# Output tiles between the block products of four feed-forward blocks, in six short stretches

## The reference

```python
def swiglu(x, w_in, w_out):          # x 512x1024, w_in 1024x5632, w_out 2816x1024
    gate, up = jnp.split(x @ w_in, 2, axis=-1)
    return (jax.nn.silu(gate) * up) @ w_out
x = x + 0.5 * rmsnorm(swiglu(rmsnorm(x, pre_g), w_in, w_out), post_g)
```

## Time and profile before

| | |
|---|---|
| median of the runs | 3464.9 us (3463.77 to 3466.04, 2 runs) |
| profiled execution | 3456.78 us, span 3455.0 us |
| TensorE clock granted, mean | 0.957 |
| TensorE busy / its weight loads | 3112.0 / 2613.2 us |
| VectorE / GpSimd / ScalarE busy | 2193.9 / 1493.2 / 1379.3 us |

### The profile page before, as it was taken

The page is one execution under the profiler, slowest core; times in us unless marked ns, Lnnn a source line. Parts: engine busy times, 40 slices in busy tenths (PEclk is TensorE's granted clock), DMA queues, the critical chain, the costliest instruction groups (busy, mean ns, idle before and its releaser), DMA issues.

```text
span 3455.0 us, 50031 instructions
## 1 busy us (share of the span) xinstructions
PE 3112.0 (90%) x20476; PEld 2613.2 (76%) x20476; DVE 2193.9 (63%) x3116; ACT 1379.3 (40%) x2398; POOL 1493.2 (43%) x1003
## 2 busy tenths in 40 slices
PE   6999999899998989898899898997989999979897
PEld 4777778678776888876777788887888885678886
DVE  2256482446648696776554959679687616486967
ACT  3242273442454343442443434344233416452433
POOL 2234315235344474454212546427456343344743
PEclk9999999999999999998778999999999999999999
DMA  5213202212111222221001122231232230112222
GB/s 222 92 53 128 91 13 63 74 45 70 44 53 61 92 81 97 98 92 56 8 2 55 42 93 92 80 104 55 88 108 69 93 102 24 42 43 93 86 87 78
DMA packets 74164, 256.74 MB, mean 74 GB/s; under 512 B 8016, under 2 KB 11216, under 8 KB 72784
## 3 DMA queue, kind: packets, MB, share of 16 engines
q1 hardware_dynamic: 73072, 248.82, 21.3%
q0 software_dynamic: 864, 4.72, 0.4%
HBM read 251.41 MB, written 2.10 MB: 73 GB/s over the span
## 4 chain that ended last, share of the span: by engine, by line
PE 66%; DVE 19%; issue 5%; ACT 4%; POOL 4%; DMA 1%; SPq 0%; ACTq 0%; DVEq 0%; POOLq 0%
PE banks L459 64%; DVE area L1539 3%; DVE w_lo L436 3%; PE banks L468 2%; POOL w_lo L425 1%; ACT w_hi L409 1%; DVE area L1510 1%; POOL w_sum L447 1%; DVE area L1528 1%; DVE w_late L436 1%; DVE w_last L430 1%; DVE area L1517 1%; POOL w_sum L445 1%; DMA area<-in_w_mod 1%; DVE area L1534 0%
## 5 line engine op out<-in xcount | busy, mean ns | idle before, releaser
L459 PE MATMUL banks<-area,w_hi 128*128 128x256 f32 (+3 forms) x6892 | 1690.8, 337 | 154.1 <-DVE w_lo L436 120.7
L459 PEld LDWEIGHTS banks<-area,w_hi 128*128 128x128 f32 (+2 forms) x6892 | 1179.8, 191 | 335.4 <-DVE w_lo L436 134.3
L459 PE MATMUL banks<-area,w_lo 128*128 128x256 f32 (+3 forms) x3446 | 1140.8, 333 | 0.0
L459 PEld LDWEIGHTS banks<-area,w_lo 128*128 128x128 f32 (+2 forms) x3446 | 659.1, 191 | 69.8
L425 POOL TENSOR_TENSOR w_lo<-w_raw,w_hi 128x1024 fp32r<-128x1024 f32 (+2 forms) x146 | 344.8, 2363 | 517.1 <-ACT w_hi L409 479.5
L459 PE MATMUL banks<-area,w_late 128*128 128x256 f32 (+2 forms) x2766 | 499.1, 334 | 30.9 <-DVE w_late L436 29.3
L459 PEld LDWEIGHTS banks<-area,w_late 128*128 128x128 f32 (+1 forms) x2766 | 419.5, 192 | 92.7 <-DVE w_late L436 34.2
L459 PE MATMUL banks<-area,area 64*64 64x32 f32 (+11 forms) x4424 | 399.9, 314 | 65.9 <-DMA area<-in_w_mod 15.7
L459 PEld LDWEIGHTS banks<-area,area 64*64 64x64 f32 (+4 forms) x4424 | 308.7, 174 | 146.1 <-issue 57.9
L409 ACT ACTIVATE w_hi<-w_raw 128x1024 fp32r<-128x1024 f32 (+2 forms) x197 | 193.2, 985 | 321.3 <-PE banks L459 199.7
L436 DVE TENSOR_TENSOR w_lo<-w_sum,w_hi 128x1024 fp32r<-128x1024 f32 x115 | 207.1, 1803 | 47.1 <-POOL w_sum L450 42.4
(11 more groups left out here) (298 smaller groups left out, 4183.3 us busy)
## 6 DMA issues: line engine op xcount, KB each, us to landing
w_raw<-in_l_ffn_w_in SPq DMA_DIRECT2D x132, 512.0 KB, 3.4
w_raw<-in_w_in SPq DMA_DIRECT2D x66, 512.0 KB, 3.5
w_raw<-in_l_ffn_w_out SPq DMA_DIRECT2D x48, 512.0 KB, 3.5
const<-in_l_ffn_w_in SPq DMA_DIRECT2D x44, 512.0 KB, 3.5
w_raw<-in_w_mod SPq DMA_DIRECT2D x32, 512.0 KB, 4.6
w_raw<-in_w_out SPq DMA_DIRECT2D x32, 320.0 KB, 2.9
w_raw<-in_l_ffn_w_out SPq DMA_DIRECT2D x24, 384.0 KB, 3.2
w_raw<-in_w_qkv SPq DMA_DIRECT2D x18, 512.0 KB, 3.3
```

The lines of the kernel that those rows point to most:

```text
L459: return e.matmul(out, lhsT, rhs, start=first, stop=stop, skip_group_check=True)
```

## The change

`FFN_PHASES` becomes six stretches of 4, 4, 4, 4, 3 and 3 pairs. Each `w_out` piece now holds two output tiles of 4 (or 3) k-steps; there are again 24 such pieces in a block, but 48 output tiles instead of 24. From the fifth pair on each unit carries one piece of the stretch before it (the last unit of a stretch of three carries two): half of the tiles stand between `p6` and `p7`, half between `p3` and `p4`, and `p4` stands behind its own unit. The units take banks 4 to 7, the output tiles 0 to 3. The last stretch's four pieces follow the last unit, the first two k-steps of four tiles ahead. The hidden tiles go around the 8 places. The rest of plain pieces is VectorE's from the fifth pair on, and so is every whole and "last" rest of the block and that of the next stage's first two pieces. The queues of ScalarE, VectorE and GpSimd are written out anew. A raw piece's buffer also waits for its plain rest.

```diff
-FFN_PHASES = ((0, 8), (8, 16), (16, 22))
+FFN_PHASES = ((0, 4), (4, 8), (8, 12), (12, 16), (16, 19), (19, 22))
+RING = 8
...
+            for j in range(FT):
+                for c in (2 * j, 2 * j + 1):
                     yield (name + "_w_in", c, True)
-                for c in range(8):
+                for p, c in pairs_behind(j):
                     yield (name + f"_w_out{p}", c, True)
+            for c in range(4):
+                yield (name + f"_w_out{len(FFN_PHASES) - 1}", c, True)
+def pairs_behind(j):
+    p = next(p for p, (j0, j1) in enumerate(FFN_PHASES) if j0 <= j < j1)
+    if p == 0:
+        return []
+    i, n = j - FFN_PHASES[p][0], FFN_PHASES[p][1] - FFN_PHASES[p][0]
+    return [(p - 1, c) for c in range(4) if min(c, n - 1) == i]
...
-                    ents.append((n, "plain"))
-                    if ents[-2][1] == "s34":
-                        ents.append((ents[-2][0], "last"))
-                    ents += [(n, "s12"), (n, "s34")]
+                    ents += [(n, "plain"), (n, "s12"), (n, "s34"), (n, "last")]
...
-        last_leads = [n + i for n in firsts for i in (2, 3, 4, 5)]
+        last_leads = [n + i for n in firsts for i in range(6)]
...
+                if (before, "plain") in ent_at:
+                    q.wait_ge(*at("weights", before, "plain"))
...
-                if (kind == "whole" and dve == (("ffn" in order[m][0] or m in last_leads) and k not in end_ents)
-                        or (kind == "plain" and not dve)):
+                if (kind == "whole" and dve == (m in last_leads or "ffn" in order[m][0])
+                        or (kind == "plain" and dve == (order[m][1] >= 2 * (DIRECT + 2)))):
...
-                if kind == "last" and dve == (k not in end_ents):
+                if kind == "last" and dve:
...
+                        name, lambda m, p=p, n=j1 - j0: [(name + f"_w_out{p}", m // 2, n)],
+                        [(self.a_hi[:, j % RING, :], self.a_lo[:, j % RING, :]) for j in range(j0, j1)], T, y_sb,
+                        self.add.squares, lambda q, k, j0=j0: q.wait_ge(*at(name, "a", j0 + k)), add=p > 0, final=final,
+                        lead=[(m, k) for m in range(4) for k in range(j1 - j0 - 1)] if final else (),
+                        free=None if p else self.left_by_pieces, base=lambda m, n=j1 - j0: m % 2 * n))
...
+            def tiles_behind(self, u, half):
+                tiles = [(p, m) for p, c in pairs_behind(u) for m in (2 * c, 2 * c + 1)]
+                n = len(tiles) // 2
+                return tiles[n:] if half else tiles[:n]
...
-                for p in range(len(FFN_PHASES)):
-                    units = self.units(p)
-                    for u in units:
-                        for name in ("p1", "p2", "p5", "p6"):
-                            self.product_pe(q, e, u, name)
-                        if u > units[0]:
-                            self.product_pe(q, e, u - 1, "p4")
-                        for name in ("p7", "p3"):
-                            self.product_pe(q, e, u, name)
-                    self.product_pe(q, e, units[-1], "p4")
-                    self.outs[p].pe(q, e)
+                steps = [out.steps(q, e) for out in self.outs]
+                for u in range(DIRECT, FT):
+                    for name in ("p1", "p2", "p5", "p6"):
+                        self.product_pe(q, e, u, name)
+                    self.tiles_pe(steps, u, 0)
+                    for name in ("p7", "p3"):
+                        self.product_pe(q, e, u, name)
+                    self.tiles_pe(steps, u, 1)
+                    self.product_pe(q, e, u, "p4")
+                self.outs[-1].pe(q, e, steps[-1])
+            def tiles_pe(self, steps, u, half):
+                for p, m in self.tiles_behind(u, half):
+                    for _ in self.outs[p].k_tiles:
+                        next(steps[p])
...
+                if u >= RING:
+                    q.wait_ge(*at(*self.outs[self.phase(u - RING)].finished()))
+                e.activation(self.a_hi[:, u % RING, :], self.a[u % 2], ACT.Copy).then_inc(
...
+                for u in range(DIRECT, FT):
+                    q.wait_ge(*at(self.tag, "product", u, "p1"))
+                    if u - 2 >= DIRECT:
+                        q.wait_ge(*at(self.tag, "c11", u - 2))
+                    e.activation(self.p1[u % 2], self.quarter(u, 0), ACT.Copy).then_inc(
+                        *sig("ffn_p1", self.tag, "p1", u))
+                    if u > DIRECT:
+                        self.a_hi_act(q, e, u - 1)
+                    else:
+                        for v in (0, 1):
+                            self.silu_act(q, e, v)
+                    q.wait_ge(*at(self.tag, "product", u, "p6"))
+                    if u - 2 >= DIRECT:
+                        q.wait_ge(*at(self.tag, "c21", u - 2))
+                    e.activation(self.u2[u % 2], self.quarter(u, 0), ACT.Copy).then_inc(
+                        *sig("ffn_u2", self.tag, "u2", u))
+                    round_one(q, e, self.ent(u, "last"))
+                    if u == DIRECT:
+                        for v in (0, 1):
+                            self.a_hi_act(q, e, v)
+                        self.silu_act(q, e, 2)
+                    elif u + 1 < FT:
+                        round_one(q, e, self.ent(u + 1, "plain"))
+                    if u + 1 < FT:
+                        round_one(q, e, self.ent(u + 1, "s12"))
+                    else:
+                        round_one(q, e, self.last_ent())
+                    if u == DIRECT:
+                        self.a_hi_act(q, e, 2)
+                    self.silu_act(q, e, u)
+                    if u + 1 < FT:
+                        round_one(q, e, self.ent(u + 1, "s34"))
+                        for k in self.tile_ents(u + 1):
+                            round_one(q, e, k)
+                    else:
+                        round_one(q, e, self.last_ent() + 1)
+                self.a_hi_act(q, e, FT - 1)
+                self.final_act(q, e)
...
+            def tiles_dve(self, q, e, u, half):
+                for p, m in self.tiles_behind(u, half):
+                    self.outs[p].evict(q, e, m, 0)
             def dve(self, q, e):
                 self.direct_dve(q, e)
+                for u in range(DIRECT, FT):
+                    sg, a = self.sg[u % 2], self.a[u % 2]
+                    if u > DIRECT:
+                        self.up_dve(q, e, u - 1)
+                        self.tiles_dve(q, e, u - 1, 1)
+                    q.wait_ge(*at(self.tag, "product", u, "p2"))
+                    q.wait_ge(*at(self.tag, "p1", u))
+                    q.wait_ge(*at(self.tag, "product", u - 2))
+                    e.tensor_tensor(self.half(sg, 0), self.quarter(u, 1), self.p1[u % 2], ADD).then_inc(
+                        *sig("ffn_quarter", self.tag, "c11", u))
+                    for k in self.tile_ents(u):
+                        rest_one(q, e, k, dve=True)
+                    if u > DIRECT:
+                        self.a_lo_dve(q, e, u - 1)
+                        rest_one(q, e, self.ent(u, "s34"), dve=True)
+                    q.wait_ge(*at(self.tag, "product", u, "p5"))
+                    q.wait_ge(*at(self.tag, "u2", u))
+                    if u - 2 >= DIRECT:
+                        q.wait_ge(*at(self.tag, "c22", u - 2))
+                    e.tensor_tensor(self.u4[u % 2], self.quarter(u, 2), self.u2[u % 2], ADD).then_inc(
+                        *sig("ffn_u4", self.tag, "u4", u))
+                    if u == DIRECT:
+                        rest_one(q, e, self.ent(u, "last"), dve=True)
+                        self.third_dve(q, e)
+                    self.tiles_dve(q, e, u, 0)
+                    q.wait_ge(*at(self.tag, "product", u, "p7"))
+                    q.wait_ge(*at(self.tag, "u4", u))
+                    q.wait_ge(*at(self.tag, "a", u - 2))
+                    e.tensor_tensor(self.half(a, 1), self.quarter(u, 3), self.u4[u % 2], ADD).then_inc(
+                        *sig("ffn_quarter", self.tag, "c22", u))
+                    if u > DIRECT:
+                        rest_one(q, e, self.ent(u, "last"), dve=True)
+                    if u == DIRECT:
+                        self.product_dve(q, e, 2)
+                        rest_one(q, e, self.ent(u + 1, "s12"), dve=True)
+                        self.a_lo_dve(q, e, 2)
+                    if u + 1 < FT and u > DIRECT:
+                        rest_one(q, e, self.ent(u + 1, "plain"), dve=True)
+                    self.gate_dve(q, e, u)
+                    if u + 1 < FT and u > DIRECT:
+                        rest_one(q, e, self.ent(u + 1, "s12"), dve=True)
+                    if u + 1 == FT:
+                        rest_one(q, e, self.last_ent(), dve=True)
+                        rest_one(q, e, self.last_ent() + 1, dve=True)
+                self.up_dve(q, e, FT - 1)
+                self.tiles_dve(q, e, FT - 1, 1)
+                self.a_lo_dve(q, e, FT - 1)
```

(25 more changed lines are left out.)

168 lines of the change are left out of this document (44 added, 124 removed).

## The result

The changed kernel takes 3339.2 us (3336.6 to 3341.9, 2 runs) against 3464.9: ratio 0.9637, 95% interval 0.9596 to 0.9679, so 3.6% faster. The forecast was 3355, range 3318 to 3425. The profiled execution took 3341.9 us, its span 3340.2, against 3456.8 before: 114.9 us less, 28.7 a block, where the sum of the forecast had 27.6. That is close, but the parts of the sum are further off than their total, and it is luck that they cancel: the units gave 7.3 us a block more than forecast, and the starts of the blocks 6.2 less.

What follows compares the result with a forecast made beforehand. The prediction saw TensorE waiting for VectorE's badly spread load in the feed-forward units. 45.3 - 7 - 18 x 0.4 - 2.5 - 1 = 27.6 us gained a block, 110 in four, gave 3355 us, range 3318 to 3425.

Steps and rivals of the forecast that it cites:

- 45.3 us a block are lost in the units: Feed-forward units before the change: 231.5 us for 19 units where 186.2 would do, the most that spreading could give.
- 0.4 us lost per unit: The 18 units with tiles after the change: TensorE still loses 0.4 us each, between 0 and 2.4.
- GpSimd's excess: VectorE operations with both inputs in SBUF, slowed beside GpSimd: 4.2 us a unit before, 2.3 to 3.2 after.
- Taken off GpSimd: the plain rest: Per unit, moving this rest to VectorE relieves GpSimd of at least 2.4 us and gives VectorE 1.2.
- 15.0 without any relief: VectorE's time per unit with no relief from GpSimd would be 15.0 us, against TensorE's 15.7 and a forecast 13.5.
- the load is there, but in the wrong place: VectorE before the change: busy 88 of 97.5 us in the second stretch, 18 of 45 in the output tiles.
- The first unit loses 5.4 now; I take 7: First unit of each block, which has no tiles: its loss goes from 5.4 us to 7 (5 to 10).
- ScalarE's order costs nothing: ScalarE's new queue order adds no loss, since ScalarE is busy for 41.4 of 97.5 us.
- The end, 2.5 us late: End of a block: GpSimd's six additions of squares end after TensorE, costing 2.5 us (0 to 5).
- 1 us for the rests: End of a block: three weight rests on VectorE behind the last eviction cost 1 us more (0 to 4).
- TensorE keeps most of the waits: Rival: VectorE still meets GpSimd at tight places, each unit loses 1.2 us (0.8 to 1.6); 3412; chance 0.20.
- Slower: Rival: late rounding of the `w_out` piece delays ScalarE's next `p1` copy in all 18 units; 3570; chance 0.06.

Runs made afterwards that it cites:

- e4_squares: Changed kernel with the last two of six additions of squares on VectorE, ahead of its three weight rests, instead of GpSimd: 3325.5 us, 0.9605.
- e7_tiles_together: Changed kernel with both output tiles of a unit between `p6` and `p7`, none ahead of `p4`: 3446.1 us, 0.9948.
- b1_plain_only: Kernel before with only the plain rests moved from GpSimd to VectorE from the sixth pair on, and the wait in SyncE's queue: 3499.0 us, 1.0107.
- e1_start: Changed kernel with ScalarE's rounding of the fourth combined input and of pair 4's plain piece put behind the first unit's `p6`: 3338.1 us, 0.9638.
- e10_first_plain: e4_squares with the plain rest of the fifth pair (pair 4) on VectorE too: 3322.8 us, 0.958.
- e12_first_order: e10_first_plain with two VectorE operations of a block's first unit, the first "s12" rest and `u4`, moved earlier: 3324.7 us, 0.9579.
- e3_load1: Changed kernel with VectorE's plain weight rest made twice in each unit that has it (17 a block): 3361.1 us, 0.9693.
- e3_load2: Changed kernel with VectorE's plain weight rest made three times in each unit that has it (17 a block): 3469.2 us, 1.0011.

## Why the prediction was right, point by point

I compare by marks in both traces: the root behind the last block (the start for the first one), ScalarE's copies of `p1` in pairs 4 and 21 (L1460, L1467 after), the next root. Means of four blocks, after less before:

```
root -> p1(4)             +8.8 us  (10.0, 8.2, 7.9, 9.0)   forecast 7 - 5.4 + 1 = +2.6
p1(4) -> p1(21)          -26.2
p1(21) -> root           -11.3
the last two together    -37.5                             forecast -(45.3 - 5.4) + 7.2 + 2.5 = -30.2
sum                      -28.7                             forecast -27.6
```
The last two go together because 12 k-steps of tiles, 8.4 us, moved from the one to the other. So the units gave 7.3 us a block more than forecast, and the starts took 6.2 of it back. That the total came out within 1.1 us a block is luck. Only the third block's start is free of other stages: the others hold a mixer or the first network, and the copy of `p1(3)` in the first block lies 6 us apart in the changed kernel and in e4_squares, whose edit begins behind it.

**"45.3 us a block are lost in the units": too little.** The window from 2360 to 2424 us does not hold five units. Its 397 matmuls are 24 fewer than 5 x 84, for `p1` and `p2` of the first unit ran before the wait of 10.4 us. With 24 x 0.1165 = 2.8 us less of work in it, 48.1 us are lost: 5.6 in what the window has of the first unit, and 42.5 in units 4 to 21, where the forecast took 45.3 - 5.4 = 39.9. This is 2.6 of the 7.3 us.

**"0.4 us lost per unit": too much.** The steady units lose nothing. From one `c22` to the next, against the pace of the steady units (15.43 us with 8 k-steps, 0.70 less or more for each), unit 18 loses 0.6 us and unit 19, behind the unit with two pieces and four tiles, 3.6 to 3.8: 4.4 us a block for the 7.2 of the forecast, another 2.8 of the 7.3. (The view of waits has 2.6 us of it in the third block.) The remaining 1.9 I can't put down to a term. The term of the sum that was mis-sized is GpSimd's excess. I had 0.45 us for each of its busy microseconds, 2.3 to 3.2 a unit. Measured against the same minima it is 26 x (1.77 - 1.21) + 26 x (1.01 - 0.69) = 22.9 us in 13 units, 1.8 us a unit, 0.27 for each busy microsecond. VectorE has 164.89 / 13 = 12.7 us a unit for the 13.5 of the forecast, all else in that sum being right. Since it is a matter of which instruction meets which, a rate from one layout doesn't carry over to another: e7_tiles_together has the same operations and 2.9 us of excess (24 x 1.11 + 24 x 0.32, over 12 units).

The Trainium skill's rule ("SBUF — State Buffer", section "Who interferes with whom": the shared port pair is an exclusive lock) is borne out by the turns in the two timelines, to within 0.2 us. The 5.2 us a unit that I worked out from it were not exceeded, but 1.8 is far below: that much is reached only where every sum of GpSimd holds up a VectorE operation of that kind for its whole length.

**"Taken off GpSimd: the plain rest": worth nothing.** By my rate VectorE would have 13.5 - 1.2 + 0.45 x 2.4 = 13.4 us with that rest back on GpSimd, as good as 13.5; it has 159.67 / 13 = 12.3, and the time is the same. The "15.0 without any relief" was a threat that did not exist. b1_plain_only shows that this part alone, in the old queue, costs 37 us. So the gain is in what is left of the change, and 107 of its 126 us hang on the second tile standing ahead of `p4` (e7_tiles_together). The other parts, `p4` behind its own unit, the stretches of 4 and 3, the whole rests on VectorE and the new queues, were not taken apart. The reason that the prediction gave first, "the load is there, but in the wrong place", was the right one.

**"The first unit loses 5.4 now; I take 7": wrong in size.** It is this step that failed. The start of a block became 8.8 us longer in the mean (7.9 in the third: 2.1 at the border, 3.5 from there until the copy of `p1(3)`, 2.3 in the unit), where the forecast had 2.6. Some 2.7 of it are `p3` and `p4` at the lower clock behind the wait for `u4`, a price that the prediction's 7 did not name. I had read the units from 2360 us on, and the first unit's wait of 10.4 us lies before it; so I never asked what ScalarE's new order, with two roundings ahead of the `p1` copy, lets GpSimd start beside VectorE's rests. "ScalarE's order costs nothing" was argued from its busy time, and holds for the steady units only. e1_start, e10_first_plain and e12_first_order together show that neither of the two other orders tried, one of ScalarE's queue and one of VectorE's, shortens the time; less work of GpSimd beside the unit shortens it by the trace (e10_first_plain), but not clear of the noise.

**"The end, 2.5 us late", and 1 us for the rests: right.** TensorE waits 2.7 us for L535 and 2.5 for L730, and then runs its next 24 matmuls at the lower of its two clocks (granted 0.51), 5.3 us for the 3.3 of before, where these waits were 0.2 and 1.5. The mechanism had one part more than I named: the rests behind the last eviction not only follow the additions, each slows the other. e4_squares got back some 10 us.

**The rivals.** "TensorE keeps most of the waits" would have needed 1.2 us a unit; e3_load1 and e3_load2 show how near it was, one and a half rests of 1.22 us more on VectorE. "Slower" by ScalarE's queue didn't happen: the copies of `p1` in the steady units follow one another at 15.4 us. Of my marks, VectorE "about 86%" was 82%, waits for the rests "under 40 us" were 39.0, and "fewer stretches of half clock" holds in the units (1.00), but not over the span, where the mean is 0.954 for 0.957.

## What to carry to other kernels

Where one engine hands over to another many times in a unit of work, spread independent work between the hand-overs before taking work off an engine: here one tile less between `p3` and `p4` cost 107 us, and giving the relief back nothing. Read the slack of a queue from the hand-over with the least room, not from its busy share: 82% ran free in one order and cost 1.3 us a unit in another. And price the first and the last unit from their own rows; what the steady unit gains can be given back there, because other engines' work comes to lie beside theirs. When an engine seems late, ask first whether it was idle: behind the unit with four tiles it was the raw weight that came late.

## What the runs showed of the hardware

VectorE operations with both inputs in SBUF and GpSimd's take turns: in the changed kernel 1.22 us became 2.32 or 3.37, two of 0.69 became 3.45, GpSimd's 1.29 became 1.86 or 2.26, while a VectorE operation that read a bank kept its 0.41 us beside GpSimd. An operation added to VectorE cost 2.1 us instead of 1.22 only because it came to lie beside GpSimd's sums (e3_load1). Waits of TensorE were followed by matmuls at 1.2 instead of 2.4 GHz: 24 at a granted clock of 0.51 behind waits of 2.7 and 2.5 us at a block's end (5.3 us instead of 3.3), and the 24 of `p3` and `p4` behind 5.0 us in the first unit (5.8 instead of 3.2). With waits of 0.9 and 3.7 us in e4_squares the clock fell too; with 0.2, 1.2 and 1.5 in the kernel before it stayed at 1.00.
